# Attention of two heads at a time: outputs made transposed in the two halves of the PSUM rows, one norm per pair, and a new order of steps

## The reference

```python
# 16 heads; 64 plain + 32 rotary query/key columns; 64 value columns; L = 16 meta + 512 tokens
q = (rms_norm(q_lat, q_a_g) @ w_q_b).reshape(bsz, L, 16, 96)
kv = (rms_norm(kv_lat, kv_a_g) @ w_kv_b).reshape(bsz, L, 16, 64 + 64)
k_nope, v = split(kv); k = concat([k_nope, broadcast(k_pe)])   # k_pe is shared by all heads
q = rms_norm(q, q_norm_g); k = rms_norm(k, k_norm_g)            # over the 96 columns of a head
q, k = rotary on the last 32 columns of each
for s, e in blocks of 128 queries:
    sc = einsum('bqhd,bkhd->bhqk', q[:, s:e], k[:, :e]) * 96**-0.5, masked to keys <= query
    p = softmax(sc)
    outs.append(einsum('bhqk,bkhd->bqhd', p, v[:, :e]))
return concat(outs).reshape(bsz, L, 16 * 64) @ w_out
```

## Time and profile before

| | us |
|---|---|
| median of 3 runs | 2634.07 (2630.02 to 2635.15) |
| the profiled execution | 2629.76 |
| its span, first to last instruction | 2627.6 |
| PE busy | 2557.0 (97% of the span) |
| DVE busy | 1223.6 (47%) |
| ACT busy | 984.8 (37%) |
| POOL busy | 1026.0 (39%) |
| mean granted TensorE clock | 0.994 of full speed |

### The profile page before, as it was taken

How to read it: one execution, slowest core, us unless ns; L and a number is a source line. 1 busy time by engine, 2 the same in 40 slices (tenths; PEclk the granted TensorE clock), 3 DMA queues, 4 the chain that set the end, 5 groups by cost and what they waited for, 6 DMA issues and landing times. The chain is left out here.

```text
span 2627.6 us, 36264 instructions
## 1 busy us (share of the span) xinstructions
PE 2557.0 (97%) x15000; PEld 2203.2 (84%) x15000; DVE 1223.6 (47%) x1745; ACT 984.8 (37%) x1504; POOL 1026.0 (39%) x759
## 2 busy tenths in 40 slices
PE   7999999999999999799999899999998999999999
PEld 5777777777777787799999899999996887788887
DVE  6454452165445413789899543111236775412211
ACT  4333333343333333344444433222335564423321
POOL 4444444334434442233333245444433010454443
PEclk9999999999999999899999999999999999999999
DMA  4233333223333332122211123222221000233232
GB/s 141 91 100 105 91 96 96 86 75 108 99 91 101 106 89 64 57 64 60 72 60 63 57 89 105 87 90 89 89 84 58 17 25 17 84 109 96 89 96 88
DMA packets 61331, 215.67 MB, mean 82 GB/s; under 512 B 8176, under 2 KB 8560, under 8 KB 61168
## 3 DMA queue, kind: packets, MB, share of 16 engines
q1 hardware_dynamic: 57248, 202.05, 25.1%
...
...
## 5 line engine op out<-in xcount | busy, mean ns | idle before, releaser
L356 POOL TENSOR_TENSOR sb_w_lo<-sb_w_raw,sb_w_hi 128x512 fp32r<-128x512 f32 x754 | 1024.8, 1381 | 1578.8 <-ACT sb_w_hi L1147 1578.7
L383 PE MATMUL psum<-sb_h_hi,sb_w_hi 128*128 128x512 f32 (+1 forms) x2648 | 814.1, 349 | 31.0 <-DVE sb_h_lo L1647 21.2
L383 PE MATMUL psum<-sb_h_lo,sb_w_hi 128*128 128x512 f32 (+1 forms) x2648 | 792.2, 341 | 0.0
L383 PE MATMUL psum<-sb_h_hi,sb_w_lo 128*128 128x512 f32 (+1 forms) x2648 | 788.8, 339 | 0.0
L1147 ACT ACTIVATE sb_w_hi<-sb_w_raw 128x1024 fp32r<-128x1024 f32 x377 | 395.7, 1054 | 631.5 <-PE psum L383 459.3
L383 PEld LDWEIGHTS psum<-sb_h_hi,sb_w_hi 128*128 128x128 f32 x2648 | 456.5, 189 | 103.4 <-issue 25.9
L383 PEld LDWEIGHTS psum<-sb_h_lo,sb_w_hi 128*128 128x128 f32 x2648 | 455.6, 189 | 59.8 <-issue 4.1
L383 PEld LDWEIGHTS psum<-sb_h_hi,sb_w_lo 128*128 128x128 f32 x2648 | 455.8, 189 | 56.0
L383 PE MATMUL psum<-sb_mix_hi,sb_w_hi 128*128 128x264 f32 (+1 forms) x1424 | 416.6, 338 | 15.5 <-POOL sb_w_lo L356 5.8
L383 PE MATMUL psum<-sb_mix_lo,sb_w_hi 128*128 128x264 f32 (+1 forms) x1424 | 411.1, 334 | 0.0
L383 PE MATMUL psum<-sb_mix_hi,sb_w_lo 128*128 128x264 f32 (+1 forms) x1424 | 409.6, 333 | 0.0
...
## 6 DMA issues: line engine op xcount, KB each, us to landing
...
```

Source lines behind the costliest of these rows:

```text
L356: low = e.tensor_tensor(g.w_lo[:, u % 4, at], g.w_raw[:, u % 2, at], g.w_hi[:, u % 4, at].bitcast(F32), ALU.subtract)
L383: mm = e.matmul(g.psum[0:m, at + b, 0:wd], w[:, slot, P * i:P * i + m], xs[:, tile, c:c + wd], start=first and n == 0, stop=last and n == 2)
```

## The change

Five things are changed together, in the attention layer only.

1. The product with the values is turned round. The values (64 columns) are now the stationary operand and the turned probabilities (128 columns) the moving one, so the output arrives transposed, head 0 in PSUM rows 0 to 63 and head 1 in rows 64 to 127, one after the other in alternation. A tile of queries of both heads is done in one group (`V_TILES`) after steps 4, 6, and steps 0 and 1 of the next pair; the turned probabilities wait in a larger buffer (`PT_AT`).
2. The outputs no longer need turning; instead the 8 columns of inverse row sums are spread by 8 matmuls with the identity as moving operand (`pe_share_turn`), copied to SBUF by ACT (`act_share_row`) and multiplied in by one DVE operation (`dve_out_scaled`).
3. The key norms of both heads are summed by one block matrix into one set of sums and go through one mean, one inverse root and one set of Newton operations (width 536) in place of two (width 532). ACT copies the raw keys once on 128 rows (`k_heads`), in place of twice on 64.
4. The order of steps alternates the heads: (h, t) = (0,0), (1,0), (0,3), (0,1), (1,1), (0,2), (1,3), (1,2). `FREED` is unchanged.
5. On ACT, the meta block's copy follows the next step's exp in place of going before it.

```diff
-STEPS = tuple((h, t, at) for h in range(2)
-              for t, at in ((0, 4 * 512), (1, 5 * 512), (3, 4 * 512 + 496), (2, 5 * 512)))
+STEPS = ((0, 0, 4 * 512), (1, 0, 5 * 512), (0, 3, 4 * 512 + 496), (0, 1, 5 * 512),
+         (1, 1, 4 * 512), (0, 2, 5 * 512), (1, 3, 4 * 512 + 496), (1, 2, 5 * 512))
+PT_AT = (5, 7, 0, 14, 5, 10, 5, 14)
+PT_FREE = (-1, -1, -1, 0, 1, 0, 2, 2)
+V_TILES = {4: (0, 0, 1), 6: (1, 3, 4), 8: (3, 2, 6), 9: (2, 5, 7)}
...
+def pe_times_v(g, e, pair, n):
+    S = g.S
+    t, first, second = V_TILES[n]
+    e.wait_ge(S["pt"], NS * pair + second + 1)
+    if t == 0 and pair:
+        e.wait_ge(S["out2"], pair)
+    for j in [*range(t + 1), QT]:
+        block = j if j < QT else t + 1
+        for h, step in ((0, first), (1, second)):
+            mm = e.matmul(g.psum[64 * h:64 * h + 64, 7, P * t:P * t + P],
+                          g.v_all[:, j, 128 * pair + 64 * h:128 * pair + 64 * h + 64],
+                          g.p_turned(step, block, 1), start=j == 0, stop=j == QT)
+    mm.then_inc(S["pv"], 1)
+
+def pe_share_turn(g, e, pair):
...
     for t in range(QT):
-        mm = e.transpose(g.psum[:, 1, P * t:P * t + P], g.out2[:, pair % 2, t, :], g.ident[:, :])
-    mm.then_inc(S["out_turned"], 1)
+        for h in range(2):
+            c = 4 * h + t
+            mm = e.matmul(g.psum[64 * h:64 * h + 64, 1, P * t:P * t + P],
+                          g.share[:, pair % 2, c:c + 1].to_broadcast([P, 64]), g.ident[:, :],
+                          start=True, stop=True)
+    mm.then_inc(S["share_turned"], 1)
...
 def act_copy_pt(g, e, i):
     S = g.S
     t = STEPS[i % NS][1]
-    e.wait_ge(S["p_turned"], i + 1)
...
+    if t == QT - 1:
+        act_copy_pt_meta(g, e, i)
...
@@ act_mla, in the loop over steps
-        if n % 4 == 3:
-            act_copy_pt_meta(g, e, i - 1)
+        if pair and n == 3:
+            act_share_row(g, e, pair - 1)
         act_exp(g, e, i)
         if i:
             act_copy_pt(g, e, i - 1)
...
-        if pair + 1 < PAIRS and n == 7:
-            act_pair_rsqrt(g, e, pair + 1, 1)
@@ pe_mla, in the loop over steps
         if i >= 1:
             pe_turn_p(g, e, i - 1)
-        if i >= 2:
-            pe_times_v(g, e, i - 2)
-        if more and 3 <= n < 7:
-            pe_pair_totals(g, e, pair + 1, (n - 3) // 2, (n - 3) % 2)
+        if n in V_TILES:
+            pe_times_v(g, e, pair, n)
+        if pair and n < 2:
+            pe_times_v(g, e, pair - 1, NS + n)
+        if more and 3 <= n < 5:
+            pe_pair_totals(g, e, pair + 1, n - 3)
         if pair and n == 2:
-            pe_out_turn(g, e, pair - 1)
+            pe_share_turn(g, e, pair - 1)
@@ after the last step
-    pe_times_v(g, e, ALL_STEPS - 2)
-    pe_mla_out(g, e, 3, range(0, 3))
-    pe_times_v(g, e, ALL_STEPS - 1)
-    pe_mla_out(g, e, 3, range(3, 7))
-    pe_out_turn(g, e, PAIRS - 1)
+    pe_times_v(g, e, PAIRS - 1, 8)
+    pe_mla_out(g, e, 3, range(0, 2))
+    pe_share_turn(g, e, PAIRS - 1)
+    pe_times_v(g, e, PAIRS - 1, 9)
+    pe_mla_out(g, e, 3, range(2, 7))
@@ dve_mla, in the loop over steps
             if n == 5:
-                dve_pair_mean(g, e, pair + 1, 0)
+                dve_pair_mean(g, e, pair + 1)
             if n == 6:
-                for part in range(1, 3):
-                    dve_pair_newton(g, e, pair + 1, 0, part)
+                for part in range(3):
+                    dve_pair_newton(g, e, pair + 1, part)
                 for part in range(2):
                     dve_pair_keys(g, e, pair + 1, 0, part)
             if n == 7:
-                dve_pair_mean(g, e, pair + 1, 1)
+                for part in range(2):
+                    dve_pair_keys(g, e, pair + 1, 1, part)
```

More of the change, by code:

```diff
@@ L950, in pe_pair_block, with pe_pair_totals @@
         mm.then_inc(S["unit"], 1)
-def pe_pair_totals(g, e, pair, h, half):
+def pe_pair_totals(g, e, pair, half):
     S = g.S
     if half == 0:
-        if h == 0:
-            e.wait_ge(S["q_squared"], pair + 1)
-            e.wait_ge(S["k_raw"], 2 * pair + 2)
-        else:
-            e.wait_ge(S["mean"], rs_qk(pair, 0))
+        e.wait_ge(S["q_squared"], pair + 1)
+        e.wait_ge(S["k_raw"], pair + 1)
     if pair == 0:
@@ L965, in pe_pair_totals @@
     bank = 2 + half
-    e.matmul(g.psum[:, bank, 0:HALF], g.head_rows[:, h, :], g.ksq[:, HALF * half:HALF * half + HALF],
+    e.matmul(g.psum[:, bank, 0:HALF], g.head_rows[:, :], g.ksq[:, HALF * half:HALF * half + HALF],
              start=True, stop=True)
-    for c in range(2):
-        t = 2 * half + c
-        mm = e.matmul(g.psum[:, bank, HALF + c:HALF + c + 1], g.square[:, h, P * t:P * t + P],
-                      g.qk_rows[:, :], start=True, stop=True)
+    for h in range(2):
+        for c in range(2):
+            t, at = 2 * half + c, HALF + 2 * h + c
+            mm = e.matmul(g.psum[:, bank, at:at + 1], g.square[:, h, P * t:P * t + P], g.qk_rows[:, :],
+                          start=True, stop=True)
     if half:
@@ L1012, in pe_turn_p @@
     e.transpose(to, p[:, 0:P], g.ident[:, :]).then_inc(S["p_turned"], 1)
-def pe_times_v(g, e, i):
+def pe_times_v(g, e, pair, n):
     S = g.S
-    pair, n = divmod(i, NS)
-    h, t, _ = STEPS[n]
-    head = 2 * pair + h
-    e.wait_ge(S["pt"], i + 1)
-    if head and n % 4 == 0:
-        e.wait_ge(S["out2"], head)
-    pt = g.pt[:, i % 2, :]
-    dst = g.psum[:, 7, 256 * h + 64 * t:256 * h + 64 * t + 64]
-    for j in range(t + 1):
-        e.matmul(dst, pt[:, P * j:P * j + P], g.v_all[:, j, 64 * head:64 * head + 64], start=j == 0,
-                 stop=False)
-    e.matmul(dst, pt[:, P * (t + 1):P * (t + 2)], g.v_all[:, QT, 64 * head:64 * head + 64],
-             start=False, stop=True).then_inc(S["pv"], 1)
-def pe_out_turn(g, e, pair):
+    t, first, second = V_TILES[n]
[10 more added lines that the diff above has]
+def pe_share_turn(g, e, pair):
     S = g.S
-    e.wait_ge(S["out2"], 2 * pair + 2)
+    e.wait_ge(S["share"], pair + 1)
     if pair + 2 < PAIRS:
@@ L1039, in pe_out_turn @@
     if pair:
-        e.wait_ge(S["mix3"], pair)
+        e.wait_ge(S["share_row"], pair)
     for t in range(QT):
-        mm = e.transpose(g.psum[:, 1, P * t:P * t + P], g.out2[:, pair % 2, t, :], g.ident[:, :])
-    mm.then_inc(S["out_turned"], 1)
+        for h in range(2):
+            c = 4 * h + t
+            mm = e.matmul(g.psum[64 * h:64 * h + 64, 1, P * t:P * t + P],
+                          g.share[:, pair % 2, c:c + 1].to_broadcast([P, 64]), g.ident[:, :],
+                          start=True, stop=True)
+    mm.then_inc(S["share_turned"], 1)
 MLA_BANKS = (0, 2, 3, 4, 5, 0, 2, 3)
@@ L1085, in pe_mla @@
     pe_v(g, e, 1, range(2, QT + 1))
-    for h in range(2):
-        for half in range(2):
-            pe_pair_totals(g, e, 0, h, half)
+    for half in range(2):
+        pe_pair_totals(g, e, 0, half)
     for k in range(6):
@@ L1492, in act_pair_keys, with act_pair_rsqrt @@
     else:
-        e.wait_ge(S["qk_total"], 2 * pair)
+        e.wait_ge(S["qk_total"], pair)
     e.activation(halves(g.ksq[:, :]), g.both(2), ACT.Square).then_inc(S["k_squared"], 1)
-    if pair >= 2:
-        e.wait_ge(S["scores2"], NS * (pair - 1))
-    for h in range(2):
-        rows = slice(64 * h, 64 * h + 64)
-        e.activation(halves(g.k2[0:64, pair % 2, h, :]), g.both(2)[rows], ACT.Copy,
-                     scale=g.col("k_norm", 1, rows)).then_inc(S["k_raw"], 1)
-def act_pair_rsqrt(g, e, pair, h):
-    act_rsqrt(g, e, rs_qk(pair, h), g.norms(g.mean2, h), g.norms(g.rinv2[pair % 2], h))
+    if pair:
+        e.wait_ge(S["k_done"], 2 * pair)
+    e.activation(halves(g.k_heads[:, :]), g.both(2), ACT.Copy,
+                 scale=g.col("k_norm", 1)).then_inc(S["k_raw"], 1)
+def act_pair_rsqrt(g, e, pair):
+    act_rsqrt(g, e, rs_qk(pair), g.mean2[:, :], g.rinv2[pair % 2][:, :])
 def act_exp(g, e, i):
@@ L1551, in act_mla @@
     act_split(g, e, U_PAIRS[1] + LEAD)
-    for h in range(2):
-        act_pair_rsqrt(g, e, 0, h)
+    act_pair_rsqrt(g, e, 0)
     act_pair_q_squares(g, e, 1)
@@ L2475, in dve_mla @@
         dve_pair_turn(g, e, 0, part)
-    dve_pair_mean(g, e, 0, 0)
-    dve_pair_mean(g, e, 0, 1)
+    dve_pair_mean(g, e, 0)
     for part in range(3):
-        dve_pair_newton(g, e, 0, 0, part)
-    for part in range(2):
-        dve_pair_keys(g, e, 0, 0, part)
+        dve_pair_newton(g, e, 0, part)
+    for h in range(2):
+        for part in range(2):
+            dve_pair_keys(g, e, 0, h, part)
     for i in range(ALL_STEPS):
```

159 lines of the change are left out of this document (87 added, 72 removed).

## The result

The changed kernel takes 2635.61 us (median of 20 executions, lowest 2632.44), the kernel before 2629.91 in the same comparison (20 executions, 2628.06 to 2635.15): ratio 1.0019, interval 1.0012 to 1.0026. It is slower by 0.2%; the medians are 5.7 us apart, where 4.8 us less were forecast. One of the twenty executions took 13763.65 us, which nothing here explains, and the ratio leaves it out. The profiled spans, 2633.8 against 2627.6, differ by 6.2 us, and that difference can be followed to its places.

A forecast was written before the change was run, and what follows sets the result against it. The pair looked bound by PE, with waits for exps. Seven pairs (-2.6 us), the layer's start (0) and the last pair and end (-2.2) gave -4.8: 2625.0 profiled, 2629 on the median; range 2618 to 2641, leaving out rivals 1 to 3.

The forecast's parts named there:

- the price of a pass and of a switch: PE's products with the values: 0.061 us a pass plus 0.1 for each of 4 groups, saving 2.1 a pair.
- rival 1: PE's value passes: the column halves do not overlap, a pass costs 0.11 us and more; 2656 us, chance 0.07.
- both new waits and the old ones that go: PE waits 0.74 us at step 6 and 2.2 at step 0; old waits at step 2 and the end go.
- the clock in the 2.2 us stretch: PE's idle gap ahead of step 0: the forecast kept the clock at 1.00 there and counted no loss.
- rival 2: Clock falls in the new 2.2 us gap: at most +5.4 a pair, up to 2667 us; chance 0.07.
- step 6 at 12.60: PE's scores of step 6 start 12.60 us after those of step 2, behind a new wait of 0.74.
- rival 4: Small unseen waits, such as ACT late at step 3, 0.4 to 1.3 us a pair; 2632 to 2641, chance 0.20.

The follow-up runs named there:

- the third experiment: Changed kernel with the rotation's second part moved two steps earlier on DVE (step 4 to step 2): 2634.87 us, ratio 1.0024 to the kernel before.
- the first experiment: Changed kernel with ACT's meta copy ahead of the exp of steps 3 and 7 again: 2628.81 us, ratio 0.9999 to the kernel before.

## Why the prediction was wrong

**Right: the price of a pass and of a switch.** PE, changed kernel (20 passes for both heads in step 0; 16 for the turn of shares; the sums; 8 passes in step 4):

```profile
2105.87 1.09 PE L1049 MATMUL psum<-sb_ident,sb_share 128*64 128x128 f32 x16
...
2106.89 0.73 PE L1000 MATMUL psum<-sb_k,sb_q 128*128 128x272 f32 x2
...
2110.06 0.70 PE L1000 MATMUL psum<-sb_k,sb_q 128*128 128x272 f32 x2
...
2111.82 0.66 PE L1032 MATMUL psum<-sb_pt,sb_v_all 128*64 128x128 f32 x8
...
2112.41 0.71 PE L972 MATMUL psum<-sb_ksq,sb_head_rows 128*128 128x264 f32 x2
...
2113.77 0.92 PE L1000 MATMUL psum<-sb_k,sb_q 128*128 128x400 f32 x2
```

And step 0 of pair 5, at the full clock:

```profile
2154.14 1.31 PE L1032 MATMUL psum<-sb_pt,sb_v_all 128*64 128x128 f32 x20
2155.38 0.51 PE L1000 MATMUL psum<-sb_k,sb_q 128*128 128x144 f32 x2
```

Twenty passes take 1.24 us (0.062 each; 0.061 forecast from the earlier trace rows), sixteen 1.02, eight 0.59 with the switch. The halves overlap, and rival 1 is out. The trace's single records show how: the passes of the two halves start 0.006 us apart (2154.410 and 2154.416), and the next two 0.109 behind them, so two passes share the time that the forecast took for the stream of one, 0.110. The Trainium skill, TensorE: Matmul & The Clock Gate, Part 3 (the mechanism), has the rule that a weight load overlaps a running matmul only in another row group; by it rival 1 would have held, with its 0.11 and more a pass. The trace disagrees, with 0.062. PE is busy 2.07 us less a pair, of 2.5 forecast.

**Right: both new waits and the old ones that go.** Step 6 of one pair to the next step 0, changed kernel (the rows that answer to the earlier trace rows):

```profile
2117.94 0.22 PE L1001 MATMUL psum<-sb_mask,sb_ident 128*128 128x128 bf16 x1
...
2122.62 0.56 DVE L2475 TENSOR_REDUCE sb_top<-psum 128x1 f32<-128x400 f32 x1
...
2123.41 0.68 ACT L1527 ACTIVATE sb_p<-psum,sb_neg_top,sb_rinv 128x400 f32<-128x400 f32 x1 [2.90 <-DVE sb_neg_top L2477]
...
2124.08 0.27 ACT L1544 ACTIVATE sb_pt<-psum 128x128 f32<-128x128 f32 x1
...
2124.49 0.57 PE L1000 MATMUL psum<-sb_k,sb_q 128*128 128x144 f32 x2 [2.11 <-ACT sb_pt L1544]
```

The maximum of step 7 starts 4.68 behind the mask of step 6 (4.6 forecast), the wait is 2.11 (2.2), step 6 to step 0 takes 7.73 (7.6), steps 0 and 1 take 5.45 at the full clock (5.38). At the end, the waits of the earlier trace rows are gone, and 2.56 us are won from step 2 of the last pair on (2.2 forecast, from its step 0); the transposes of the last step wait 0.42 (0.6).

**Wrong, the step that failed: the clock in the 2.2 us stretch stood in the sum with nothing, as rival 2 with a chance of 0.07.** It fell, in four of six pairs of the profile, and cost 7.1 us with the fall at the start: more than the whole gain forecast. The mechanism was priced as an upper bound (5.4 a pair, all of steps 0 and 1 at half speed); measured are 1.57, since the clock comes back on the way: in the slow pair of 2124.49 the matmuls from step 1's scores (2128.99) to the next step 2 (2131.51) take 2.52 us, as in the fast one (2155.38 to 2157.90). The chance was read from a single stretch of 2.16 us in the earlier trace rows behind which the clock stood at full. I took that row for a property of the length. It was one draw, and the trace of the kernel before had a draw that went the other way, in a part that the change doesn't touch. PE of the kernel before behind a stretch of 2.35 us, and the window from there (granted clock 0.62):

```profile
525.74 0.77 PE L383 MATMUL psum<-sb_h_hi,sb_w_hi 128*128 128x512 f32 x1 [2.35 <-DVE sb_h_lo L1647]
...
525.74:529.74 4.00, 4.00 (x10) 2.86 (x11) 3.93 (x7) 1.25 (x3) 0.00 (x0) 0.62 0.00 0
```

That trace has six stretches of 2.1 to 2.9 us behind its first 30 us, and the low clock followed this one of them. One in six, seven times 1.57, is an estimate of 1.8 us that the record of before would have supported, and it was taken as nothing. Even that would have been too little: of 18 stretches of 2.1 us in three profiles of the new order 11 brought the low clock, which for the six stretches of an execution makes 5.8 us, and the forecast no gain.

**Wrong too: step 6 at 12.60.** The period at full clock is 26.40, not 25.6, and the seven periods together are 5.3 us longer than forecast, nearly as much as the clock cost; alone it would have made a gain of 4.8 into nothing. Of the 0.8 in a middle period, 0.60 is the way from step 2 to the scores of step 6 (13.20). PE's share of it is 0.25: the scores of step 5 start 10.21 behind those of step 2, not 9.96, mostly in step 4 (3.71 us for 3.51). DVE's is 0.35, and it has a cause that the forecast didn't see. POOL, DVE, ACT and PE in step 5 of pair 3, changed kernel:

```profile
2110.86 0.44 DVE L2475 TENSOR_REDUCE sb_top<-psum 128x1 f32<-128x272 f32 x1 [1.39 <-PE psum L1001]
2110.91 2.51 POOL L365 TENSOR_TENSOR sb_w_lo<-sb_w_raw,sb_w_hi 128x512 fp32r<-128x512 f32 x2 [23.89 <-ACT sb_w_hi L1159]
...
2111.33 0.87 DVE L2477 SCALAR_TENSOR_TENSOR sb_neg_top<-sb_top,sb_rinv 128x1 f32<-128x1 f32 x1
...
2112.23 2.26 DVE L2417 TENSOR_TENSOR sb_q<-sb_q,sb_scaled 32x1024 f32<-32x1024 f32 x1
...
2114.53 0.69 DVE L2501 TENSOR_TENSOR sb_mix_lo<-sb_share_row,sb_mix_hi 128x512 fp32r<-128x512 f32 x1
...
2115.14 0.57 DVE L2475 TENSOR_REDUCE sb_top<-psum 128x1 f32<-128x400 f32 x1
...
2116.76 0.40 PE L997 MATMUL psum<-sb_k,sb_q 128*128 128x16 f32 x2 [0.94 <-ACT sb_p L1527]
```

The same steps in pair 0 (second profile of the same kernel), where no weights are split and no outputs divided:

```profile
2030.08 0.16 DVE L2477 SCALAR_TENSOR_TENSOR sb_neg_top<-sb_top,sb_rinv 128x1 f32<-128x1 f32 x1
...
2030.27 1.22 DVE L2417 TENSOR_TENSOR sb_q<-sb_q,sb_scaled 32x1024 f32<-32x1024 f32 x1
...
2035.16 0.40 PE L997 MATMUL psum<-sb_k,sb_q 128*128 128x16 f32 x2 [0.59 <-ACT sb_p L1527]
```

Beside POOL's subtraction the scaling of one column takes 0.87 for 0.16 and the last operation of the rotation 2.26 for 1.22, so the maximum of step 5 comes late, and the wait is 0.94 instead of 0.59. In the kernel before, POOL's pair started when that rotation was already running, DVE paid nothing, and POOL took 2.91 for 2.51:

```profile
2107.80 1.22 DVE L2390 TENSOR_TENSOR sb_q<-sb_q,sb_scaled 32x1024 f32<-32x1024 f32 x1
...
2108.48 2.91 POOL L356 TENSOR_TENSOR sb_w_lo<-sb_w_raw,sb_w_hi 128x512 fp32r<-128x512 f32 x2 [23.06 <-ACT sb_w_hi L1147]
```

The Trainium skill, SBUF — State Buffer, Who interferes with whom, has this as a rule: a VectorE instruction with two SBUF inputs contends with a GpSimd one that reads SBUF, and which of them is issued first decides which one is blocked. The trace agrees: the maximum at 2110.86, which reads PSUM, keeps its 0.44. Which of the two starts first was turned round by the new order: the rotation's last operation stands behind the maximum of step 4, which now ends later than POOL's start.

That the rotation's place is what costs the 0.35 is shown by the third experiment. The division of the outputs (L2501) stayed there ahead of the maximum of step 5, and DVE still stood idle before that maximum:

```profile
2087.35 0.69 DVE L2501 TENSOR_TENSOR sb_mix_lo<-sb_share_row,sb_mix_hi 128x512 fp32r<-128x512 f32 x1 [1.64 <-ACT sb_mix_hi L1570]
...
2088.28 0.57 DVE L2475 TENSOR_REDUCE sb_top<-psum 128x1 f32<-128x400 f32 x1 [0.24 <-PE psum L1001]
```

The wait at step 6 is 0.58 there, as in pair 0. With the rotation in its place that operation can be slowed too: in the first experiment and in that with the keys behind the maximum the rotation takes 2.19 and L2501 1.64, and the wait at step 6 is 1.10.

Small terms make up the rest: 0.13 between step 6 and step 0, 0.07 in steps 0 and 1. Together they are what rival 4 described (0.4 to 1.3 a pair), so the time came out as rivals 2 and 4 at once, each of which had been taken alone. That the measured 2635.61 lies inside the stated range, 2618 to 2641, is luck: the range leaves rival 2 out, and only because a fall costs 1.57 us and not 5.4 did the time stay inside it.
